# Attention tiles of a two-layer transformer kernel: two tiles of look-ahead, a stacked rope query, joined context tiles, narrower weight splits

## The chip, the cores and the metric

One NeuronCore of a Trainium2 chip runs the whole program. The metric is the device time in microseconds (us) of one execution.

## The reference, cut to what matters

Two layers act on 512 latent tokens (`h`) and 256 context tokens (`g`), model width 1024, in float32. Each layer is: gated feed-forward, a mixer, gated feed-forward, each behind a modulated RMS norm. Layer 0's mixer is the attention in question; layer 1's is a retention, and layer 1 updates only the latents in the end.

```
q = qk_norm(rms_norm(cq) @ w_uq)            # 8 heads, 128 "nope" + 64 "rope" columns
k = qk_norm(rms_norm(ckv) @ w_ukv), k_rope shared by all heads
s = einsum(q, k) * 192 ** -0.5              # nope part + rope part
p = softmax(s); y = (p @ v) @ w_o
# latents: 512 queries over 768 keys (context and latents)
# context: 256 queries over the 256 context keys
```

## The kernel before, in words

Everything is held transposed (features on partitions, tokens along the free dimension). To keep float32 accuracy at the fast matmul format, each operand is split into a high part, rounded by ScalarE (ACT), and a low part, the rest, computed by VectorE (DVE). `three()` (L303) then issues three matmuls: low x high, high x low, high x high. Weights stream in units of 128x2048 through two slots `s0`, `s1`: SyncE loads `raw[s]`, ACT's `split_hi` (L888) writes `wh[s]`, DVE's `split_lo` (L1271) writes `wl[s]` and signals `w_ready[s]`, on which TensorE (PE) waits and after which SyncE loads the next unit.

There is no planner: the order of work is written out by hand in one block for each engine, and semaphores tie the blocks together. The attention stands in `pair()`, once in each block, for four pairs of heads. A pair has three stages.

1. **Items.** PE projects five items (rope queries of both heads, nope queries of each head, nope keys of each head: `project`) and the values. Each item is copied and squared by ACT (`item_square`), summed by PE (`item_sum`, L319), rooted by ACT (`root`), inverted by DVE (`inverse`, L1564), spread over the partitions by PE (`item_spread`, L333), scaled by DVE (`scaled`, L1570), and split (`hi` L1068, `lo` L1576). The rope query of both heads is one tile: head 0 on partitions 0 to 63, head 1 on 64 to 127. It takes one `hi` and one `lo`, into `qrr[:, 0]` and `qrr[:, 1]`. The rope key `krr` holds the same 64 rows twice, and is made once.
2. **Tiles.** Twelve tiles of 128 queries: for each head context queries 4 and 5, then latent queries 0 to 3. Of each tile: `scores` (PE, a `three` of 128 rows and a `three` of the 64 rope rows for each bank of keys); `maximum` (DVE, L1614); `exponent` (ACT, L1113, into one of two rows of `nrm`, with the sum); `diagonal` (DVE, L1621 and L1622, the identity times 1/sum); `turn` (PE, L625, transposes and weights by a matmul with that diagonal); `turned` (ACT L1119 and L1121, then DVE L1627 and L1630, the split of the result into `pt`). `weigh` multiplies by the values, `attended` splits the output. PE issues scores one tile ahead of `turn`; scores of tile n+2 reuse the PSUM banks of tile n and wait for `exp_done` of n; every `turn` waits for `pt_ready` of the tile before it.
3. **Output.** `project_out` for 8 blocks of 512 latents over three PSUM banks, added into `h` by DVE (L1373), then `project_ctx`. `wo_used`, after its first half, lets ACT split the next pair's first unit. PE waits for that unit's `w_ready` at the start of the next pair.

The attention's weight units fill 1152, 1024 or 1024 of the 2048 columns (query, key/value and output weights); some splits are already `1024` wide, others take all 2048.

Of the kernel before, what the change touches and what calls it, by code (L numbers as in the profile page):

```python
# [54 lines left out]
W_BANKS = (0, 3, 2, 5)  # L55
# [48 lines left out]
def build(nc, weights, ada0, ada, c_rows, vecs, consts, x_in, rope_mla, rope_ret, dist_in, out):  # L104
    with ExitStack() as ctx:
# [23 lines left out]
        row = sb("row", [P, 3, 2])  # L129
# [59 lines left out]
        vv = [t[:, 3072:4608].rearrange("p (k e) -> p k e", k=6) for t in xf]  # L189
        oo = [t[:, 4608:6144].rearrange("p (j t) -> p j t", j=2) for t in xf]  # L190
# [108 lines left out]
        def _(pe):  # L299
# [302 lines left out]
            tiles = [(hh, q) for hh in range(2) for q in (4, 5, 0, 1, 2, 3)]  # L602

            def scores(n, hh, q):

                if n >= 2:
                    pe.wait_ge(exp_done, c.next(exp_done))
                b = 2 * (n % 2)
                qs = slice(q * P, q * P + P)
                for t0, n_key in (STREAMS if q < 4 else STREAMS[1:]):  # L610
                    bank = ps[:, b + (t0 > 0), 0:n_key]
                    ks = slice(t0, t0 + n_key)
                    half = slice(ROPE * hh, ROPE * hh + ROPE)
                    three(bank, (qn[:, 0, hh, qs], qn[:, 1, hh, qs]), (kn[:, 0, hh, ks], kn[:, 1, hh, ks]), True, False)
                    ins = three(bank, (qrr[:, 0, qs], qrr[:, 1, qs]), (krr[:, 0, ks], krr[:, 1, ks]), False, True, half)
                ins.then_inc(s_full, 1)

            def turn(n, hh, q):


                pe.wait_ge(p_done, c.next(p_done))
                if n >= 1:
                    pe.wait_ge(pt_ready, c.next(pt_ready))
                for kc in (range(6) if q < 4 else (4, 5)):
                    ins = mm(ps[:, 4 + kc // 4, (kc % 4) * P:(kc % 4) * P + P], nrm[:, n % 2, kc * P:kc * P + P],  # L625
                             nrm[:, 2, (n % 2) * P:(n % 2) * P + P], start=True, stop=True)
                ins.then_inc(pt_full, 1)

            def weigh(hh, part):

                keys = (4, 5) if part == 2 else range(6)
                q0, bank, at = ((0, 6, 0), (L, 6, L), (L, 7, 0))[part]
                for kc in keys:
                    ins = three(ps[:, bank, at:at + L], (vv[0][:, kc, hh * DV:hh * DV + DV], vv[1][:, kc, hh * DV:hh * DV + DV]),
                                (pt[0][:, kc, q0:q0 + L], pt[1][:, kc, q0:q0 + L]), kc == keys[0], kc == keys[-1])
                if part:
                    ins.then_inc(o_full, 1)
# [3 lines left out]
            def pair(first=False, last=False):  # L641
# [52 lines left out]
                scores(0, *tiles[0])  # L694
                for n, (hh, q) in enumerate(tiles):
                    if n == 5:
                        pe.wait_ge(item_ready, c.next(item_ready))
                    if n + 1 < len(tiles):
                        scores(n + 1, *tiles[n + 1])
# [3 lines left out]
                    if q == 1:  # L703
                        weigh(hh, 2)
                    if q == 3:
                        weigh(hh, 0)
                    if q == 4 and hh == 1:
                        pe.wait_ge(pt_ready, c.ahead(pt_ready, 1))
                        weigh(0, 1)
                    turn(n, hh, q)  # L710
                    if q == 0 and hh == 1:
                        pe.wait_ge(o_ready, c.next(o_ready, 2))

                def project_out(m, kk):

                    if kk == 0 and m >= 3:
                        pe.wait_ge(y_added, c.next(y_added))
                    ins = three(ps[:, A_BANKS[m % 3], :], w((s0, s1)[kk], m * P),
# [20 lines left out]
                for m, kk in ((0, 1), (1, 1)) + tuple((m, kk) for m in range(2, KD) for kk in range(2)):  # L739
                    project_out(m, kk)  # L740
                for odd in range(2):
# [8 lines left out]
                c.next(y_added, 3)  # L750
# [5 lines left out]
            with c.loop(pe, PAIRS - 2, {w_ready[0]: 2, w_ready[1]: 2, item_v: 5, item_sq: 5, item_inv: 5,  # L756
                                        item_ready: 5, item_rot: 1, v_ready: 3, exp_done: 12, p_done: 12, pt_ready: 12, o_ready: 4,
# [126 lines left out]
        def _(act):  # L884
# [203 lines left out]
            split_hi(s1)  # L1088
# [10 lines left out]
            split_hi(s0)  # L1099
# [6 lines left out]
            tiles = [(hh, q) for hh in range(2) for q in (4, 5, 0, 1, 2, 3)]  # L1106

            def exponent(n, hh, q):
                act.wait_ge(max_done, c.next(max_done))
                b, e = n % 2, n % 2  # L1110
                cols = (0, T) if q < 4 else (S, T)
                flat = ps[:, 2 * b:2 * b + 2, :].rearrange("p b t -> p (b t)")
                fn(nrm[:, e, cols[0]:cols[1]], flat[:, cols[0]:cols[1]], ACT.Exp, bias=row[:, 0, b:b + 1],  # L1113
                   accum_out=row[:, 1, b:b + 1]).then_inc(exp_done, 1)

            def turned(n, hh, q):
                act.wait_ge(pt_full, c.next(pt_full))
                if q < 4:
                    fn(pt[0][:, 0:4, q * P:q * P + P], ps[:, 4, :].rearrange("p (k q) -> p k q", k=4), ACT.Copy)  # L1119
                q0 = q * P if q < 4 else L + (q - 4) * P  # L1120
                fn(pt[0][:, 4:6, q0:q0 + P], ps[:, 5, 0:256].rearrange("p (k q) -> p k q", k=2), ACT.Copy  # L1121
                   ).then_inc(pt_hi, 1)
# [8 lines left out]
            def pair(first=False, last=False):  # L1131
# [10 lines left out]
                hi(qrr[:, 0, :], nrm[:, 0, :], item_rot)  # L1142
# [15 lines left out]
                exponent(0, *tiles[0])  # L1158
                hi(kn[:, 0, 1, :], nrm[:, 1, :])
                c.next(item_ready, 3)  # L1160
                for n, (hh, q) in enumerate(tiles):
                    if n + 1 < len(tiles):
                        exponent(n + 1, *tiles[n + 1])
                    if q == 1:
                        attended(hh, 1)
                    if q == 4 and hh == 1:
                        attended(0, 0)
                    turned(n, hh, q)
                    if n == 2:
                        split_hi(s1, 1024)  # L1170
# [5 lines left out]
                split_hi(s0)  # L1176
                act.wait_ge(y_full, c.next(y_full, 2 * KD))
                split_hi(s1)

            pair(first=True)  # L1180
            with c.loop(act, PAIRS - 2, {item_full: 5, item_ms: 5, item_v: 5, item_ready: 5, item_rot: 1, v_full: 3, max_done: 12,
                                         pt_full: 12, o_full: 4, wo_used: 1, y_full: 16, raw_full[0]: 32, raw_full[1]: 32}):
                pair()
# [83 lines left out]
        def _(dve):  # L1267
# [117 lines left out]
            def last_y(layer, k, s, parts=STREAMS, early=None):  # L1385

                coefs(layer, k)
                for m in range(KD):
                    add_part(m, parts[0], A_BANKS[m % 3])
# [196 lines left out]
            split_lo(s1)  # L1586
# [9 lines left out]
            for k in range(3):  # L1596
                if k < 2:
                    scaled(k, g[:, k:k + 1], k == 0, pre_kv)
                if k == 1:
                    split_lo(s0)  # L1600
# [6 lines left out]
            tiles = [(hh, q) for hh in range(2) for q in (4, 5, 0, 1, 2, 3)]  # L1607

            def maximum(n, hh, q):
                dve.wait_ge(s_full, c.next(s_full))  # L1610
                b = n % 2
                cols = (0, T) if q < 4 else (S, T)
                flat = ps[:, 2 * b:2 * b + 2, :].rearrange("p b t -> p (b t)")
                nc.vector.tensor_reduce(row[:, 0, b:b + 1], flat[:, cols[0]:cols[1]], AX_X, ALU.max, negate=True  # L1614
                                        ).then_inc(max_done, 1)

            def diagonal(n, hh, q):

                dve.wait_ge(exp_done, c.next(exp_done))
                b = n % 2  # L1620
                step(nc.vector.reciprocal(row[:, 2, b:b + 1], row[:, 1, b:b + 1]))  # L1621
                ts(nrm[:, 2, b * P:b * P + P], ident, row[:, 2, b:b + 1], None, ALU.mult).then_inc(p_done, 1)  # L1622

            def turned(n, hh, q):
                dve.wait_ge(pt_hi, c.next(pt_hi))
                if q < 4:
                    tt(pt[1][:, 0:4, q * P:q * P + P], ps[:, 4, :].rearrange("p (k q) -> p k q", k=4),  # L1627
                       pt[0][:, 0:4, q * P:q * P + P].bitcast(F32), ALU.subtract)
                q0 = q * P if q < 4 else L + (q - 4) * P
                tt(pt[1][:, 4:6, q0:q0 + P], ps[:, 5, 0:256].rearrange("p (k q) -> p k q", k=2),  # L1630
                   pt[0][:, 4:6, q0:q0 + P].bitcast(F32), ALU.subtract).then_inc(pt_ready, 1)
# [9 lines left out]
            def pair(first=False, last=False):  # L1641
# [8 lines left out]
                lo(qrr[:, 1, :], qrr[:, 0, :], nrm[:, 0, :])  # L1650
# [17 lines left out]
                maximum(0, *tiles[0])  # L1668
                value(2)
                for n, (hh, q) in enumerate(tiles):  # L1670
                    diagonal(n, hh, q)
                    if n == 0:
                        lo(kn[:, 1, 1, :], kn[:, 0, 1, :], nrm[:, 1, :])
                    if n + 1 < len(tiles):
                        maximum(n + 1, *tiles[n + 1])
                    if n == 2:
                        split_lo(s0, 1024)
                    if n == 4:
                        split_lo(s1, 1024)
                    if q == 1:  # L1680
                        attended(hh, 1)
                    if q == 4 and hh == 1:
                        attended(0, 0)
                    turned(n, hh, q)
# [4 lines left out]
                for m in range(KD):  # L1689
                    add_part(m, STREAMS[0], A_BANKS[m % 3])  # L1690
                add_pair(0, STREAMS[1], W_BANKS)
                split_lo(s0)
                for m in (2, 4, 6):
                    add_pair(m, STREAMS[1], W_BANKS)
                split_lo(s1)

            pair(first=True)
            with c.loop(dve, PAIRS - 2, {item_std: 5, item_hi: 5, item_swapped: 1, v_hi: 3, s_full: 12, exp_done: 12,
                                         pt_hi: 12, o_hi: 4, y_full: 16, w_hi[0]: 2, w_hi[1]: 2, item_rms: 5,
# [252 lines left out]
```

## Time and profile before

| | before |
|---|---|
| median of 3 runs | 3191.51 us (3191.02 to 3193.46) |
| the profiled execution's own time | 3189.59 us |
| its span, first to last instruction | 3187.9 us |
| PE busy | 3075.0 us, 96% |
| DVE busy | 1820.9 us, 57% |
| ACT busy | 864.7 us, 27% |
| attention, pairs 1 to 4 | about 679 to 1109 us of the span |

Lines of a timeline are: start in us, duration in us, engine, line, operation, operands, count, and in brackets the idle time of the engine before it with what ended it. Durations of pipelined matmuls overlap, so the distance from start to start is the cost in a stream. `wl`, `xnl` and so on name memory, which the attention reuses: `xnh`/`xnl` hold `pt`, the values and the attention output.

### The profile page before, as it was taken

Reading aid. Unit: us, or ns where it says so; the run is one execution under the profiler, and the core shown is the slowest. Engines: PE = TensorE matmul, PEld = TensorE weight load, DVE = VectorE, ACT = ScalarE, POOL = GpSimd, SP = SyncE. Lnnn points to the kernel's source line nnn. Section 1 sums busy time; section 2 is a strip of 40 time slices with the busy share of each in tenths; the row PEclk is TensorE's granted clock in tenths of the full one; section 3 lists DMA queues with packets and bytes.
Section 4 is the critical chain, followed back from the end, with each engine's and each line's share of the span. In section 5 each row is a group of like instructions: output and inputs, shape, how many; then the busy total and the mean of one; then the engine's idle time right before and its main releaser. Section 6 shows DMA issues by size and latency. Waiting matters only on the chain.

```text
span 3187.9 us, 42477 instructions
## 1 busy us (share of the span) xinstructions
PE 3075.0 (96%) x17592; PEld 2638.7 (83%) x17592; DVE 1820.9 (57%) x2652; ACT 864.7 (27%) x1188; POOL 36.7 (1%) x73
## 2 busy tenths in 40 slices
PE   6999999999999899999999999999899999999999
PEld 4888888877777788888888888888788888888887
DVE  4675565864565576655565365656654546454444
ACT  3211121343443431111223111112322223242221
POOL 0000000000000000000000000000000000000000
PEclk8999999999999999999999999999899999999999
DMA  6332322111010043323221132322111212122222
GB/s 241 133 132 99 112 105 92 53 47 53 27 53 27 30 156 119 119 93 118 105 92 54 66 110 97 112 106 87 53 48 59 79 39 79 40 80 94 97 94 84
DMA packets 40984, 277.81 MB, mean 87 GB/s; under 512 B 4352, under 2 KB 5632, under 8 KB 8000
## 3 DMA queue, kind: packets, MB, share of 16 engines
q1 hardware_dynamic: 31024, 205.85, 17.8%
q0 software_dynamic: 9872, 70.72, 6.2%
q8 instruction: 64, 1.05, 0.1%
q14 instruction: 24, 0.20, 0.0%
HBM read 274.45 MB, written 2.10 MB: 87 GB/s over the span
## 4 chain that ended last, share of the span: by engine, by line
PE 90%; DVE 6%; ACT 2%; issue 1%; DMA 0%; SPq 0%; DVEq 0%; ACTq 0%
PE ps L305 29%; PE ps L306 28%; PE ps L307 28%; PE ps L625 2%; PE ps L333 1%; DVE wl L1273 1%; ACT wh L891 1%; DVE act_buf L1357 1%; DVE xnl L1361 1%; PE ps L319 0%; DMA ada_w<-ada 0%; PE ps L351 0%; ACT xnh L922 0%; DVE nrm L1570 0%; PE ps L418 0%
## 5 line engine op out<-in xcount | busy, mean ns | idle before, releaser
L305 PE MATMUL ps<-xnh,wl 128*128 128x512 f32 (+1 forms) x3040 | 1062.5, 350 | 31.4 <-DVE wl L1273 15.6
L306 PE MATMUL ps<-xnl,wh 128*128 128x512 f32 (+1 forms) x3040 | 1052.3, 346 | 0.0
L307 PE MATMUL ps<-xnh,wh 128*128 128x512 f32 (+1 forms) x3040 | 1051.7, 346 | 0.0
L305 PEld LDWEIGHTS ps<-xnh,wl 128*128 128x128 f32 x3040 | 580.7, 191 | 113.7 <-DVE wl L1273 17.5
L307 PEld LDWEIGHTS ps<-xnh,wh 128*128 128x128 f32 x3040 | 580.9, 191 | 70.8
L306 PEld LDWEIGHTS ps<-xnl,wh 128*128 128x128 f32 x3040 | 581.2, 191 | 68.2 <-issue 1.0
L1273 DVE TENSOR_TENSOR wl<-raw,wh 128x2048 fp32r<-128x2048 f32 (+1 forms) x183 | 410.3, 2242 | 145.3 <-ACT wh L891 145.1
L891 ACT ACTIVATE wh<-raw 128x2048 fp32r<-128x2048 f32 (+1 forms) x178 | 332.7, 1871 | 578.8 <-PE ps L307 578.8
L1415 DVE SCALAR_TENSOR_TENSOR h<-ps,coef,h 128x512 f32<-128x512 f32 x624 | 371.7, 642 | 116.1 <-PE ps L307 115.5
L305 PE MATMUL ps<-hidh,wl 128*128 128x512 f32 (+1 forms) x1232 | 425.0, 345 | 3.1 <-DVE h L1373 3.1
L306 PE MATMUL ps<-hidl,wh 128*128 128x512 f32 (+1 forms) x1232 | 426.0, 346 | 0.0
L307 PE MATMUL ps<-hidh,wh 128*128 128x512 f32 (+1 forms) x1232 | 425.2, 345 | 0.0
L1427 DVE TENSOR_TENSOR act_buf<-act_buf,ps 128x512 f32<-128x512 f32 x88 | 60.5, 687 | 542.1 <-ACT act_buf L968 417.0
L966 ACT ACTIVATE act_buf<-ps 128x512 f32<-128x512 f32 x88 | 52.6, 598 | 911.7 <-PE ps L307 911.6
L305 PEld LDWEIGHTS ps<-hidh,wl 128*128 128x128 f32 x1232 | 231.3, 188 | 36.5 <-DVE h L1373 4.4
L306 PEld LDWEIGHTS ps<-hidl,wh 128*128 128x128 f32 x1232 | 231.4, 188 | 31.6
L307 PEld LDWEIGHTS ps<-hidh,wh 128*128 128x128 f32 x1232 | 231.1, 188 | 31.2
L1286 DVE CUSTOM_DVE_ANT_0 ada_prod<-adaw,c_act 128x1024 f32<-128x1024 f32 x120 | 146.5, 1221 | 2.7 <-ACT c_act L895 1.7
L1286 DVE CUSTOM_DVE_ANT_0 adaw<-adaw,c_act 128x1024 f32<-128x1024 f32 x120 | 146.3, 1219 | 0.0
L305 PE MATMUL ps<-wh,xnl 128*128 128x256 f32 x384 | 109.9, 286 | 12.6 <-DVE rv L1754 12.6
L1432 DVE TENSOR_TENSOR hidl<-act_buf,hidh 128x768 fp32r<-128x768 f32 (+1 forms) x88 | 78.5, 892 | 75.6 <-ACT hidh L971 75.6
L306 PE MATMUL ps<-wl,xnh 128*128 128x256 f32 x384 | 109.3, 285 | 0.0
(233 smaller groups left out, 3056.9 us busy)
## 6 DMA issues: line engine op xcount, KB each, us to landing
raw<-weights SPq DMA_DIRECT2D x183, 1024.0 KB, 4.8
adaw<-ada POOLq DMA_DIRECT2D x64, 1024.0 KB, 5.0
ada_w<-ada SPq DMA_DIRECT2D x8, 1024.0 KB, 20.0
h<-x_in SPq DMA_DIRECT2D x1, 2048.0 KB, 8.6
c_act<-c_rows POOLq DMA_DIRECT2D x2, 1024.0 KB, 5.1
out<-h SPq DMA_DIRECT2D x8, 256.0 KB, 2.0
h<-x_in SPq DMA_DIRECT2D x1, 1024.0 KB, 28.9
cs<-rope_mla POOLq DMA_DIRECT2D x1, 512.0 KB, 3.5
```

The costliest lines, as they stand in the source:

```text
L305: mm(dst, lhs[1][rows], rhs[0][rows], start=first, stop=False)
L306: mm(dst, lhs[0][rows], rhs[1][rows], start=False, stop=False)
L307: return mm(dst, lhs[0][rows], rhs[0][rows], start=False, stop=last)
L333: ins = mm(ps[m * i:m * i + m, bank, a - t0:b - t0], quarter[:, col:col + 1].to_broadcast([P, m]), inv[:, a - g * n:b - g * n], start=True ...
L625: ins = mm(ps[:, 4 + kc // 4, (kc % 4) * P:(kc % 4) * P + P], nrm[:, n % 2, kc * P:kc * P + P], nrm[:, 2, (n % 2) * P:(n % 2) * P + P], st ...
L891: fn(wh[:, s, 0:n], raw[:, s, 0:n], ACT.Copy).then_inc(w_hi[s], 1)
L966: ins = fn(act_buf[:, j, 0:S], ps[:, 3 * j, :], ACT.Silu)
L1273: tt(wl[:, s, 0:n], raw[:, s, 0:n], wh[:, s, 0:n].bitcast(F32), ALU.subtract).then_inc(w_ready[s], 1)
L1286: ins = nc.vector.tensor_tensor_reduce(out=prod, in0=w, in1=c_act[:, j, :], scale=1.0, scalar=0.0, op0=ALU.mult, op1=ALU.add, accum_out=ad ...
L1415: ins = stt(out=h[:, m, t0:t0 + n], in0=ps[:, bank, 0:n], scalar=coef[:, 1, m, i:i + 1], in1=h[:, m, t0:t0 + n], op0=ALU.mult, op1=ALU.add)
L1427: ins = tt(act_buf[:, j, 0:S], act_buf[:, j, 0:S], ps[:, 3 * j + 1, :], ALU.mult)
L1432: tt(hidl[:, par, j, 0:n_tok], act_buf[:, j, 0:n_tok], hidh[:, par, j, 0:n_tok].bitcast(F32), ALU.subtract).then_inc(hid_ready, 1)
```

## The change

- `TILES` has ten entries instead of twelve: a head's two context tiles become one, with one set of banks, one `maximum` instruction, two exponentials, two diagonals, four `turn` matmuls and one copy of each half, into its own memory `ptc` (an unused tail of weight slot 0).
- Scores of tiles 0 and 1 are issued before the loop and those of n+2 in it; the exponentials rotate through three rows (`p_row`). ACT and DVE do `exponent(n+2)`, `maximum(n+2)`, `diagonal(n+1)` around `turned(n)`.
- The rope query is stacked: for head hh, `qrr[:, hh]` holds the high part in the head's own 64 partitions and the low part in the other 64. Two matmuls over 128 rows (key low, key high) take the place of three over 64 rows. The split takes two `hi` and two `lo` instructions.
- `weigh` of latent halves is split in two groups of three key blocks, placed behind other turns.
- `project_out` rotates over four banks, and four of its first halves are issued early instead of two.
- Splits of attention units are 3*384 = 1152 or 1024 wide throughout.

```diff
+TILES = [(hh, q) for hh in range(2) for q in (4, 0, 1, 2, 3)]
+        def p_row(n):
+            return (nrm[:, 0, :], sqb[:], nrm[:, 1, :])[n % 3]
...
-                    ins = three(bank, (qrr[:, 0, qs], qrr[:, 1, qs]), (krr[:, 0, ks], krr[:, 1, ks]), False, True, half)
+                    mm(bank, qrr[:, hh, qs], krr[:, 1, ks], start=False, stop=False)
+                    ins = mm(bank, qrr[:, hh, qs], krr[:, 0, ks], start=False, stop=True)
...
-                scores(0, *tiles[0])
-                for n, (hh, q) in enumerate(tiles):
-                    if n == 5:
+                for n in range(2):
+                    scores(n, *TILES[n])
+                for n, (hh, q) in enumerate(TILES):
+                    if n == 3:
                         pe.wait_ge(item_ready, c.next(item_ready))
-                    if n + 1 < len(tiles):
-                        scores(n + 1, *tiles[n + 1])
+                    if n + 2 < len(TILES):
+                        scores(n + 2, *TILES[n + 2])
                     if n == 0:
                         pe.wait_ge(v_ready, c.next(v_ready, 2))
                         pe.wait_ge(item_v, c.next(item_v))
-                    if q == 1:
-                        weigh(hh, 2)
-                    if q == 3:
-                        weigh(hh, 0)
-                    if q == 4 and hh == 1:
-                        pe.wait_ge(pt_ready, c.ahead(pt_ready, 1))
-                        weigh(0, 1)
-                    turn(n, hh, q)
-                    if q == 0 and hh == 1:
-                        pe.wait_ge(o_ready, c.next(o_ready, 2))
+                    turn(n, hh, q)
+                    if n in (6, 8):
+                        pe.wait_ge(o_ready, c.ahead(o_ready, 1))
+                    if n in (3, 8):
+                        weigh(hh, 0, range(0, 3))
+                    if n in (4, 9):
+                        weigh(hh, 0, range(3, 6))
+                    if n == 5:
+                        weigh(0, 1, range(0, 3))
+                    if n == 6:
+                        weigh(0, 1, range(3, 6))
+                    if n in (1, 6):
+                        weigh(hh, 2)
...
                 project_out(0, 0)
+                project_out(2, 0)
                 pe.wait_ge(pt_ready, c.next(pt_ready))
                 weigh(1, 1)
                 project_out(1, 0)
+                project_out(3, 0)
...
-                hi(qrr[:, 0, :], nrm[:, 0, :], item_rot)
+                act.wait_ge(item_rot, c.next(item_rot))
+                for hh in range(2):
+                    own = slice(ROPE * hh, ROPE * hh + ROPE)
+                    ins = fn(qrr[own, hh, :], nrm[own, 0, :], ACT.Copy)
+                ins.then_inc(item_hi, 1)
...
+                exponent(1, *TILES[1])
+                for n, (hh, q) in enumerate(TILES):
+                    turned(n, hh, q)
+                    if n + 2 < len(TILES):
+                        exponent(n + 2, *TILES[n + 2])
+                    if n == 2:
+                        attended(0, 1)
+                        split_hi(s1, 1024)
+                    if n == 7:
+                        attended(0, 0)
+                        attended(1, 1)
...
-                split_hi(s0)
+                split_hi(s0, 3 * 384)
...
+                lo(kn[:, 1, 1, :], kn[:, 0, 1, :], nrm[:, 1, :])
+                maximum(1, *TILES[1])
+                diagonal(0, *TILES[0])
+                for n, (hh, q) in enumerate(TILES):
+                    if n + 2 < len(TILES):
+                        maximum(n + 2, *TILES[n + 2])
+                    if n + 1 < len(TILES):
+                        diagonal(n + 1, *TILES[n + 1])
+                    turned(n, hh, q)
+                    if n in (1, 3):
+                        split_lo((s0, s1)[n // 2], 1024)
```

## Rows read from the trace of the kernel before

**Rows 1.** The page: busy us, share and instructions of each engine.

```profile
PE 3075.0 (96%) x17592; PEld 2638.7 (83%) x17592; DVE 1820.9 (57%) x2652; ACT 864.7 (27%) x1188; POOL 36.7 (1%) x73
```

**Rows 2.** Windows: length; PE, PEld, DVE, ACT, POOL busy; PEclk; DMA share, GB/s.

```profile
780.00:790.00 10.00, 7.11 (x38) 6.25 (x38) 7.72 (x10) 3.71 (x2) 0.00 (x0) 0.83 0.32 105
...
1000.00:1010.00 10.00, 7.03 (x45) 5.71 (x44) 6.84 (x8) 5.38 (x7) 0.00 (x0) 1.00 0.44 133
...
928.00:985.00 57.00, 52.56 (x325) 41.45 (x324) 30.34 (x66) 21.81 (x51) 0.00 (x0) 1.00 0.10 37
```

**Rows 3.** Waits of PE, 676 to 1130 us: total us, times, longest.

```profile
PE ps L305 <- DVE wl L1273: 13.1, 4, 4.3
PE ps L305 <- DVE xnl L1630: 9.8, 8, 1.3
PE ps L625 <- DVE nrm L1622: 5.3, 8, 0.8
...
PE ps L305 <- DVE xnl L1636: 3.0, 4, 0.8
```

**Rows 4.** Timeline of PE: one latent tile's scores, a turn, context scores, weighing.

```profile
943.67 0.48 PE L305 MATMUL ps<-kn,qn 128*128 128x512 f32 x1
...
945.44 0.38 PE L305 MATMUL ps<-kn,qn 128*128 128x256 f32 x1
...
946.53 1.60 PE L625 MATMUL ps<-nrm 128*128 128x128 f32 x12
947.89 0.36 PE L305 MATMUL ps<-kn,qn 128*128 128x256 f32 x1
...
948.97 0.39 PE L305 MATMUL ps<-xnh,xnl 128*128 128x256 f32 x1
```

**Rows 5.** Timeline of PE: first projection after a pair boundary, and the next.

```profile
1003.04 0.51 PE L305 MATMUL ps<-cqn,wl 128*128 128x512 f32 x1 [2.97 <-DVE wl L1273]
...
1006.31 0.39 PE L305 MATMUL ps<-cqn,wl 128*128 128x512 f32 x1
```

**Rows 6.** Timeline of PE: a turn, and the weighing that waits for its split.

```profile
951.23 1.50 PE L625 MATMUL ps<-nrm 128*128 128x128 f32 x12
...
954.74 0.39 PE L305 MATMUL ps<-xnh,xnl 128*128 128x256 f32 x1 [1.12 <-DVE xnl L1630]
```

**Rows 7.** Lines by form, 928 to 985 us: count, busy us, mean ns, idle before.

```profile
L1614 DVE TENSOR_REDUCE row<-ps 128x1 f32<-128x768 f32 x8 | 7.7, 958 | 2.5 <-PE ps L307 2.5
...
L1273 DVE TENSOR_TENSOR wl<-raw,wh 128x1024 fp32r<-128x1024 f32 x2 | 2.4, 1214 | 0.0
...
L1113 ACT ACTIVATE nrm<-ps,row 128x256 f32<-128x256 f32 x4 | 1.9, 475 | 6.0 <-DVE row L1614 6.0
...
L891 ACT ACTIVATE wh<-raw 128x1024 fp32r<-128x1024 f32 x1 | 1.1, 1067 | 0.0
```

**Rows 8.** Timeline of PE and DVE: the first tile's scores, and its maximum.

```profile
927.76 0.42 PE L305 MATMUL ps<-kn,qn 128*128 128x256 f32 x1
...
929.15 0.41 DVE L1614 TENSOR_REDUCE row<-ps 128x1 f32<-128x256 f32 x1
```

**Rows 9.** Timeline of all engines: the rope query's split, and the next spread.

```profile
912.93 0.84 ACT L1068 ACTIVATE qrr<-nrm 128x768 fp32r<-128x768 f32 x1 [1.09 <-DVE nrm L1583]
...
913.80 0.96 DVE L1576 TENSOR_TENSOR qrr<-nrm,qrr 128x768 fp32r<-128x768 f32 x1 [0.91 <-ACT qrr L1068]
...
915.80 1.35 DVE L1564 RECIPROCAL irms<-irms 128x192 f32<-128x192 f32 x1
...
917.31 1.59 PE L333 MATMUL ps<-irms,mats 128*128 128x192 f32 x10
```

**Rows 10.** Timeline of ACT and DVE: splits at the end of pair 3.

```profile
998.75 3.71 ACT L891 ACTIVATE wh<-raw 128x2048 fp32r<-128x2048 f32 x2 [15.02 <-PE ps L307]
...
1000.70 2.29 DVE L1273 TENSOR_TENSOR wl<-raw,wh 128x2048 fp32r<-128x2048 f32 x1 [0.79 <-ACT wh L891]
```

**Rows 11.** Timeline of PE: the spread at the start of pair 1.

```profile
676.40 2.65 PE L333 MATMUL ps<-irms,mats 128*128 128x192 f32 x10 [1.88 <-DVE irms L1564]
```

More of the change, by code:

```diff
@@ L128, in build @@
         lg = sb("lg", [P, 7, 8])
-        row = sb("row", [P, 3, 2])
+        row = sb("row", [P, 3, 2, 2])
         eps = sb("eps", [P, 1])
@@ L600, in _ @@
             slot = s1
-            tiles = [(hh, q) for hh in range(2) for q in (4, 5, 0, 1, 2, 3)]
             def scores(n, hh, q):
@@ L736, in pair @@
                 project_out(1, 0)
+                project_out(3, 0)
                 pe.wait_ge(w_ready[s1], c.next(w_ready[s1]))
                 pe.wait_ge(o_ready, c.next(o_ready, 2))
-                for m, kk in ((0, 1), (1, 1)) + tuple((m, kk) for m in range(2, KD) for kk in range(2)):
+                for m, kk in tuple((m, 1) for m in range(4)) + tuple((m, kk) for m in range(4, KD) for kk in range(2)):
                     project_out(m, kk)
+                pe.wait_ge(y_added, c.next(y_added, 2))
                 for odd in range(2):
@@ L749, in pair @@
                         project_ctx(m, 1)
-                c.next(y_added, 3)
+                c.next(y_added, 2)
                 if not last:
@@ L1104, in _ @@
             slot = s1
-            tiles = [(hh, q) for hh in range(2) for q in (4, 5, 0, 1, 2, 3)]
             def exponent(n, hh, q):
                 act.wait_ge(max_done, c.next(max_done))
[L1110 to L1114, printed above, removed]
+                b = n % 2
+                if q < 4:
+                    flat = ps[:, 2 * b:2 * b + 2, :].rearrange("p b t -> p (b t)")
+                    ins = fn(p_row(n), flat[:, 0:T], ACT.Exp, bias=row[:, 0, b, 0:1], accum_out=row[:, 1, b, 0:1])
+                else:
+                    for i in range(2):
+                        ins = fn(p_row(n)[:, L * i:L * i + L], ps[:, 2 * b + i, 0:L], ACT.Exp, bias=row[:, 0, b, i:i + 1],
+                                 accum_out=row[:, 1, b, i:i + 1])
+                ins.then_inc(exp_done, 1)
             def turned(n, hh, q):
@@ L1157, in pair @@
                 value(2)
-                exponent(0, *tiles[0])
+                exponent(0, *TILES[0])
                 hi(kn[:, 0, 1, :], nrm[:, 1, :])
                 c.next(item_ready, 3)
[L1161 to L1166, printed above, removed]
+                exponent(1, *TILES[1])
[7 more added lines that the diff above has]
+                    if n == 7:
                         attended(0, 0)
-                    turned(n, hh, q)
-                    if n == 2:
-                        split_hi(s1, 1024)
+                        attended(1, 1)
                 attended(1, 0)
@@ L1388, in last_y @@
                 for m in range(KD):
-                    add_part(m, parts[0], A_BANKS[m % 3])
+                    add_part(m, parts[0], A_BANKS[m % 3] if early is None else O_BANKS[m % 4])
                     if m >= 2:
@@ L1605, in _ @@
             slot = s1
-            tiles = [(hh, q) for hh in range(2) for q in (4, 5, 0, 1, 2, 3)]
             def maximum(n, hh, q):
@@ L1611, in maximum @@
                 b = n % 2
[L1612 to L1615, printed above, removed]
+                if q < 4:
+                    out_, in_ = row[:, 0, b, 0:1], ps[:, 2 * b:2 * b + 2, :].rearrange("p b t -> p (b t)")[:, 0:T]
+                else:
+                    out_, in_ = row[:, 0, b, :], ps[:, 2 * b:2 * b + 2, 0:L]
+                nc.vector.tensor_reduce(out_, in_, AX_X, ALU.max, negate=True).then_inc(max_done, 1)
             def diagonal(n, hh, q):
                 dve.wait_ge(exp_done, c.next(exp_done))
-                b = n % 2
-                step(nc.vector.reciprocal(row[:, 2, b:b + 1], row[:, 1, b:b + 1]))
-                ts(nrm[:, 2, b * P:b * P + P], ident, row[:, 2, b:b + 1], None, ALU.mult).then_inc(p_done, 1)
+                b, parts = n % 2, 1 if q < 4 else 2
+                step(nc.vector.reciprocal(row[:, 2, b, 0:parts], row[:, 1, b, 0:parts]))
+                for i in range(parts):
+                    at = (2 * b + i) * P
+                    ins = ts(nrm[:, 2, at:at + P], ident, row[:, 2, b, i:i + 1], None, ALU.mult)
+                ins.then_inc(p_done, 1)
             def turned(n, hh, q):
@@ L1649, in pair @@
                 rotated(0)
-                lo(qrr[:, 1, :], qrr[:, 0, :], nrm[:, 0, :])
+                dve.wait_ge(item_hi, c.next(item_hi))
+                for hh in range(2):
+                    own, other = (slice(ROPE * g, ROPE * g + ROPE) for g in (hh, 1 - hh))
+                    ins = tt(qrr[other, hh, :], nrm[own, 0, :], qrr[own, hh, :].bitcast(F32), ALU.subtract)
+                ins.then_inc(item_ready, 1)
                 scaled(1, gate_cols["qg_nope"])
@@ L1667, in pair @@
                 scaled(1, gate_cols["kg_nope"])
-                maximum(0, *tiles[0])
+                maximum(0, *TILES[0])
                 value(2)
[L1670 to L1675, printed above, removed]
-                    if n == 2:
[L1677 to L1682, printed above, removed]
+                lo(kn[:, 1, 1, :], kn[:, 0, 1, :], nrm[:, 1, :])
[9 more added lines that the diff above has]
+                        split_lo((s0, s1)[n // 2], 1024)
+                    if n == 2:
+                        attended(0, 1)
+                    if n == 7:
                         attended(0, 0)
-                    turned(n, hh, q)
+                        attended(1, 1)
                 attended(1, 0)
```

89 lines of the change are left out of this document (52 added, 37 removed).

## The prediction, made before the changed kernel ran

> **What bounds the kernel now.** I read the page's busy times first: PE is busy 96% of the span and no other engine is near that [rows 1]. So a change pays by PE work that it removes, or by PE waits. The change touches only the four attention pairs, so I then took the windows. A pair's tile stage lasts about 57 us, and in it PE is busy 52.6, DVE 30.3 and ACT 21.8 [rows 2]. The reader should see there that PE is the bound of this stage too, with 4 to 5 us of waiting. The waits of PE name these [rows 3]: over four pairs 9.8 us for a turned tile's split (L1630), 5.3 for a diagonal (L1622), 3.0 for an attention output (L1636) and 13.1 for weights (L1273; three pair boundaries of about 2.9 and one of 4.3 before the next feed-forward). The last view is the timeline of PE, for what one tile costs.
>
> **Scores.** One latent tile runs from 943.67 to 946.53, 2.86 us, and one context tile from 947.89 to 948.97, 1.08 us [rows 4]. A plain stream, without the 64-row form, makes nine matmuls of 512 columns and nine of 256 in 1003.04 to 1006.31, 3.27 us, of which about 0.11 is the first one's start; one of each is (3.27 - 0.11) / 9 = 0.351 us [rows 5]. Twelve matmuls at that rate would be 6 x 0.351 = 2.11, so the tile has a surplus of 0.75: the six matmuls of the first bank alone, 943.67 to 945.44, take 1.77 [rows 4] against 6 x 0.234 = 1.40, and the 64-row form is what sets them apart from a plain stream. After the change a latent tile has five matmuls for each bank, all over 128 rows: 5 x 0.351 + 0.08 for its start = 1.83. I take the surplus as gone, since tensors change elsewhere without it: saved 1.03 a tile, 8.2 for eight. The context tiles go from 4 x 1.08 = 4.3 to two of ten 256-column matmuls at a third of 0.351, 2 x (1.17 + 0.1) = 2.5: saved 1.8. Together 10.0 us a pair. The turns keep their matmuls (a latent turn is 946.53 to 947.89, 1.36 us [rows 4]), and so does the weighing, whose four groups become seven: 3 x 0.1 = 0.3 lost.
>
> **Waits in the tile stage.** Before, a pair waits 9.8/4 + 5.3/4 + 3.0/4 (the last attention output, L1636) = 4.5 us [rows 3]. The new ones follow from one length: a latent turn starts at 951.23, its split is ready at 954.74 [rows 6]. That is 3.5, less the turn's own 1.25 to 1.36, so 2.25 us must be covered by other PE work between two turns. In the new order it is covered by scores (1.83) and half a weighing (9 matmuls of 256 columns, 1.1 to 1.2) for most turns. It is not before turn 3 (context scores alone, 1.27: waits 1.0), before turn 8 (nothing: waits 2.25) and before turn 9 (half a weighing: 1.1). Behind a context turn the split is one ACT and one DVE instruction, about 1.5, and scores cover it. The end, attended output against two early `project_out` halves instead of one, leaves about 0.15 of 0.75.
>
> The start is worse than now. Scores 0 start at 927.76 and DVE's first maximum at 929.15, since the item before it has to be scaled first [rows 8]. From there the new order runs on DVE and ACT: maximum of 512 columns about 0.7 (768 take 0.96 [rows 7]), two exponentials 2 x 0.475 [rows 7], key `hi` 0.83 and `lo` 0.96 (the same forms as the rope query's 0.84 and 0.96 [rows 9]), maximum 1 0.96, reciprocal and two diagonals about 0.8, hand-overs 0.1: 5.3. So turn 0 can start 1.4 + 5.3 = 6.7 us after scores 0. PE has 1.27 + 2 x 1.83 = 4.9 to do: it waits 1.8. The sum of new waits is 1.8 + 1.0 + 2.25 + 1.1 + 0.15 = 6.3, which is 1.8 more than now.
>
> DVE's own load stays below PE's: a latent tile costs it 0.96 + 0.5 + 1.0 = 2.5 against PE's 1.83 + 1.36 + 1.1. The third exponential row lets `exponent(n+2)` be written while `turn(n)` may still read row n; with this order it is a condition, and I cost it at nothing. The splits of the output weights sit on DVE (1.2 each [rows 7]) behind turned 1 and 3, where scores and weighing cover them; without that cover each would cost its 1.2. Four output banks instead of three cost and save nothing, as none of PE's waits here is on an addition [rows 3]. The new wait for two additions ahead of the context projection has two later blocks, 12 x 0.234 = 2.8 us, to hide it; what stands behind it is that projection and the next pair.
>
> **The rope query's split.** Two `hi` instead of one, and two `lo` after both. ACT's takes 0.84 and ends at 913.77, DVE's starts at 913.80 and takes 0.96 [rows 9]; half the partitions do not shorten such an instruction if its time goes by its 768 columns, which no row here shows. That bounds the cost between 0 (time goes by partitions) and 0.84 + 0.96 = 1.8. What is next late is the spread at 917.31 [rows 9]: the inverse that it needs ran from 915.80 to 917.15, ending 0.16 before it [rows 9]. So nearly all arrives at PE, and I take 1.6.
>
> A pair therefore gains 10.0 - 0.3 - 1.8 - 1.6 = 6.3, four pairs 25.2 us.
>
> **Narrower splits.** At the end of a pair ACT splits two full units in 3.71, 1.86 each, and DVE takes 2.29 [rows 10]; at 1024 columns they take 1.07 and 1.21 [rows 7]. At 1152 that makes 1.2 and 1.37: 0.66 + 0.92 = 1.6 a boundary, all of it inside PE's wait of 2.97 [rows 5], which remains with 1.4. Three boundaries: 4.8. Ahead of pair 1 a full split becomes 1024 wide in front of the inverse for which PE waits 1.88 [rows 11]: 0.8 + 1.08, taken as 1.8. The wait of 4.3 before the feed-forward is a full unit's and stays. DMA moves the same units.
>
> **The clock.** Around the first boundary the granted clock averages 0.83 over 10 us [rows 2], that is a third of it at 1.2 GHz and the rest at 2.4, at a price of about 1.7 us; the second boundary shows the same and the third (1.00 [rows 2]) does not, though PE idles equally. Shorter boundary gaps may give back 3; the new waits of 1.8 and 2.25 may cause falls of their own. I take two such falls against two saved: nothing.
>
> **Sum.** 25.2 + 4.8 + 1.8 = 31.8. The profiled execution took 3189.6 and would take 3157.8; the median shown is 1.9 above it, so 3159.5.
>
> **The rivals.**
> 1. *Less waiting than I wrote* (0.17). The split by halves may be half as long, and the first maximum may run early. Without the rope cost (6.4) and the start's wait (7.2) the time is 3146. For: PE's order leaves room in both. Against: the two orders of DVE and ACT are fixed.
> 2. *Turned splits late* (0.15). On DVE `maximum(n+2)` and `diagonal(n+1)` stand in front of `turned(n)`, and on ACT `exponent(n+1)`. If they are not done when a turn ends, 2.25 becomes up to 3.7. That would add 0.7 at five covered turns and 1.45 at three bare ones, 7.9 a pair: 31 in all, no gain left. At half of that the time is 3175. Against: by the rows these instructions have been released when the turn starts.
> 3. *The surplus of the scores stays* (0.06). If 0.75 a tile belongs to something else than the 64-row form, scores save only a matmul a bank: 8 x 0.351 + 4 x 0.117 = 3.3 a pair. Then pairs lose 0.4 each and 3186.5 remains, within what can be told from no change. The Trainium skill (TensorEngine Tiling (Array Packing), Key Properties) says that changing the tiling mode drains TensorE, which speaks against this rival. The same page (Theoretical Speedup) says that a contraction of up to 64 rows can run up to twice as fast. By that, three 64-row matmuls would cost 1.5 full ones, fewer than the two that replace them, and scores would lose 0.18 a tile. The trace disagrees: the 64-row threes are longer, not shorter.
> 4. *The clock falls* (0.04), and the result is slower. Place: the tail of each pair, where waits of 2.25, 1.1 and 1.4 now follow each other. Each us of work at 1.2 GHz loses half a us. The point of decision is 2 x (31.8 + 6.4) / 4 = 19 us a pair at the lower level. With all of the 36 us from turn 8 to the next pair's first projections at 1.2 GHz, 18 x 4 = 72 is lost and the time is 3231. Against: in the tile stage the clock stays at 1.00 through waits of up to 1.3 [rows 2, 3]. The Trainium skill (TensorE: Matmul & The Clock Gate, A second HAM failure mode) describes this, frequent short idles between groups of matmuls that make the clock oscillate; here only falls beside the longer waits are seen.
>
> **The numbers.** The forecast has 0.58, its own range 3152 to 3167 (rope split 0 to 1.8, some falls more or fewer). The whole range, 3146 to 3176, takes in rivals 1 and the half of 2. About 0.2%, 6.4 us, is what a measurement of this kernel tells from no change. Faster by more: forecast, 1 and 2, 0.90; within: rival 3, 0.06; slower: rival 4, 0.04.
>
> **What would show it.** Right: a latent tile's scores in 1.8 us with even steps of 0.234 and 0.117; PE waits of about 1.8 on L1622's successor once a pair, about 2.25 once; boundary waits near 1.4; a new wait of about 1.5 ahead of a spread in the item stage. Wrong: more than 8 us of waits in a tile stage (rival 2), scores still above 2.3 (rival 3), PEclk below 0.9 in tile windows (rival 4), or rope copies of 0.5 us (rival 1).

## The result, and the profile after

The changed kernel takes 3135.35 us (median of 4 runs, 3134.22 to 3136.25); the kernel before, measured beside it, 3191.9. The ratio is 0.9823, 95% interval 0.9807 to 0.9838. Forecast were 3159.5 and 3146 to 3176: the direction is right, the gain of 56 us is far more than the 32 forecast. The span of the profiled execution fell from 3187.9 to 3134.2, by 53.7 us.

The page answers to [rows 1] with:

```profile
PE 3019.6 (96%) x17512; PEld 2624.0 (84%) x17512; DVE 1811.6 (58%) x2632; ACT 859.2 (27%) x1184; POOL 36.7 (1%) x73
```

Where the time went is best read by cutting both traces at the same matmuls. The attention stretch runs from the last matmul of the first feed-forward on its hidden activations (`hidh`) to the first such one of the next feed-forward:

| stretch, in us | before | after | less | forecast |
|---|---|---|---|---|
| first matmuls to 606.86 / 605.12 | 606.9 | 605.1 | 1.7 | 0 |
| the attention stretch, to 1186.93 / 1144.69 | 580.1 | 539.6 | 40.5 | 31.8 |
| the three feed-forwards and the retention behind it, to the start of the last matmul | 1997.4 | 1985.9 | 11.5 | 0 |

So 13 us are saved in code that the diff does not touch, and 9 more than forecast in the attention. The windows of the attention stretch, with columns as in [rows 2], divide its part. First the kernel before, then the changed one:

```profile
606.86:1186.93 580.07, 535.64 (x3339) 439.73 (x3338) 352.31 (x588) 240.02 (x462) 4.20 (x8) 0.98 0.15 54
605.12:1144.69 539.57, 494.03 (x3259) 430.22 (x3258) 343.22 (x568) 234.44 (x458) 4.21 (x8) 0.98 0.16 58
```

PE is busy 41.6 us less, where the forecast's terms make 38.8, and idle 1.1 us more, where they make 7.0. So of the 9 us about 6 are waits that did not come, and 3 are PE work.

The timeline of PE in the third pair shows that the tiles themselves came out as worked out:

```profile
900.90 0.41 PE L311 MATMUL ps<-kn,qn 128*128 128x256 f32 x1
...
907.50 0.68 PE L635 MATMUL ps<-nrm 128*128 128x128 f32 x4 [1.26 <-DVE nrm L1653]
...
908.39 0.48 PE L311 MATMUL ps<-kn,qn 128*128 128x512 f32 x1
...
910.23 1.50 PE L630 MATMUL ps<-nrm,sqb 128*128 128x128 f32 x12
...
917.64 1.58 PE L630 MATMUL ps<-nrm 128*128 128x128 f32 x12 [0.92 <-DVE xnl L1660]
...
938.25 2.13 PE L630 MATMUL ps<-nrm 128*128 128x128 f32 x12 [2.11 <-DVE xnl L1660]
...
965.59 0.51 PE L311 MATMUL ps<-cqn,wl 128*128 128x512 f32 x1 [1.29 <-DVE wl L1303]
```

A latent tile's scores take 910.23 - 908.39 = 1.84 us (forecast 1.83, before 2.86). Turn 0 starts 6.6 after scores 0 (forecast 6.7). Turns 3 and 8 wait 0.92 and 2.11 (1.0 and 2.25), the boundary 1.29 (1.4). The waits of PE, 600 to 1110 us, answer to [rows 3]; columns are us in total, times, longest. The five waits for `wl` take in one of 0.9 us ahead of pair 1, which the window of [rows 3] leaves out:

```profile
PE ps L630 <- DVE xnl L1660: 13.9, 12, 2.1
PE ps L311 <- DVE wl L1303: 8.9, 5, 4.3
PE ps L339 <- DVE irms L1594: 8.6, 8, 1.8
PE ps L635 <- DVE nrm L1653: 5.0, 4, 1.3
```

### The profile page after: what moved, and what is told of

Same layout as the page of the kernel before. It is cut to its first block, busy times and chain, and to the rows that moved or that the text cites. A ratio compares the mean times of both kernels' runs of the same rounds, so it can differ in the third digit from the quotient of the medians.

```text
span 3134.2 us, 42265 instructions
## 1 busy us (share of the span) xinstructions
PE 3019.6 (96%) x17512; PEld 2624.0 (84%) x17512; DVE 1811.6 (58%) x2632; ACT 859.2 (27%) x1184; POOL 36.7 (1%) x73
## 4 chain that ended last, share of the span: by engine, by line
PE 88%; DVE 7%; ACT 2%; issue 2%; DMA 0%; SPq 0%; DVEq 0%; ACTq 0%
PE ps L311 28%; PE ps L313 28%; PE ps L312 28%; PE ps L630 2%; PE ps L339 1%; DVE wl L1303 1%; DVE act_buf L1387 1%; ACT wh L913 1%; DVE xnl L1391 1%; DVE irms L1594 0%; PE ps L325 0%; DVE ssum L1366 0%; DMA ada_w<-ada 0%; PE ps L357 0%; ACT xnh L944 0%
## 5 line engine op out<-in xcount | busy, mean ns | idle before, releaser
L1303 DVE TENSOR_TENSOR wl<-raw,wh 128x2048 fp32r<-128x2048 f32 (+2 forms) x183 | 402.3, 2199 | 142.0 <-ACT wh L913 141.7
L913 ACT ACTIVATE wh<-raw 128x2048 fp32r<-128x2048 f32 (+2 forms) x178 | 326.7, 1835 | 564.8 <-PE ps L313 564.8
```

The costliest lines, as they stand in the source:

```text
L913: fn(wh[:, s, 0:n], raw[:, s, 0:n], ACT.Copy).then_inc(w_hi[s], 1)
L1303: tt(wl[:, s, 0:n], raw[:, s, 0:n], wh[:, s, 0:n].bitcast(F32), ALU.subtract).then_inc(w_ready[s], 1)
```

## The experiments

Labels e1 to e12 are runs of their own; times are medians of 4 to 7 runs, each beside 9 to 11 runs of the kernel before on the same chip (3189.8 beside e1 to e4, 3191.4 beside e5 to e8, 3191.5 beside e9 to e12).

**The 13 us outside.** In feed-forward code both programs issue the same matmuls. The timeline of PE in the second feed-forward, before:

```profile
1599.95 0.28 PE L305 MATMUL ps<-hidh,wl 128*128 128x256 f32 x1
...
1600.30 0.39 PE L305 MATMUL ps<-hidh,wl 128*128 128x512 f32 x1
...
1600.99 0.39 PE L305 MATMUL ps<-hidh,wl 128*128 128x512 f32 x1
```

and after:

```profile
1599.93 0.39 PE L311 MATMUL ps<-hidh,wl 128*128 128x512 f32 x1
...
1600.62 0.28 PE L311 MATMUL ps<-hidh,wl 128*128 128x256 f32 x1
...
1600.96 0.28 PE L311 MATMUL ps<-hidh,wl 128*128 128x256 f32 x1
...
1601.30 0.39 PE L311 MATMUL ps<-hidh,wl 128*128 128x512 f32 x1
```

Three 256-column matmuls take 0.35 us before and 0.34 after, three of 512 columns 0.69 each time here. Over all of them the median distance falls from 117 to 113 ns (256 columns) and from 233 to 229 (512), while the same matmuls on the normalised activations (`xnh`, `xnl`; xn below) stay at 120 and 227. One thing differs: `row` grew from 24 to 48 bytes a partition, and every tensor allocated after it starts 32 bytes further in memory (adding up the allocations, `hidh` starts 64 bytes past a multiple of 128 instead of 32); `xnh` and the weights stand before it.

```diff
         row = sb("row", [P, 3, 2])
+        pad = sb("pad", [P, 8])
```

> The kernel before with one unused tensor of 32 bytes a partition behind `row`, so that every tensor allocated after `row` starts 32 bytes further, as in the changed kernel; nothing else. Theory A (placement): the part of the gain that shows outside the attention, about 12 us, comes from the new shape of `row`, which moves the hidden activations, the retention's scores and the attention's queries and keys from starts that are 32 bytes past a multiple of 64 to multiples of 64; matmuls that stream them then run about 2% closer together. It expects 12 to 20 us less than before, 3172 to 3180, with the distance between hidden-activation matmuls falling from about 187 to 184 ns. Rival B (the two programs differ by where their code lies, or by the executions compared): within 3 us of before.

Measured: 3177.6, ratio 0.996 (0.9947 to 0.9974), 12.2 us less. The attention stretch stays (580.5 against 580.1), what is behind it falls from 1997.4 to 1986.0, as in the changed kernel, and the distances are its 113 and 229. Theory A holds at its lower end.

> The changed kernel with the same unused 32 bytes behind `row`, which puts the later tensors back to starts 32 bytes past a multiple of 64. Theory A expects it 12 to 20 us slower than the changed kernel, 3147 to 3155. Rival B expects 3135.

Measured: 3154.0 (the same `pad` in the changed kernel), 18.7 us more than the changed kernel; 119 and 232 ns. So 32 bytes of placement alone are worth 12 us in one program and 19 in the other. The two steps are not the same one: e1 goes from 32 to 64 bytes past a multiple of 128, e2 from 64 to 96, and not back to 32.

**The rope query.** e3 is the changed kernel with the old rope lines of the diff on PE, ACT and DVE; e4 the kernel before with the new ones.

```diff
-                    mm(bank, qrr[:, hh, qs], krr[:, 1, ks], start=False, stop=False)
-                    ins = mm(bank, qrr[:, hh, qs], krr[:, 0, ks], start=False, stop=True)
+                    half = slice(ROPE * hh, ROPE * hh + ROPE)
+                    ins = three(bank, (qrr[:, 0, qs], qrr[:, 1, qs]), (krr[:, 0, ks], krr[:, 1, ks]), False, True, half)
```

> The changed kernel with the rope query as before: one high and one low copy, three matmuls over 64 rows for each bank. By the prediction's sum the stack saves 8 x 1.03 + 1.8 = 10.0 us less 1.6 a pair of matmul time and copies, so that without it the time is up to 34 us longer, 3169; since longer scores also cover waits of 0.9 and 1.3 us a pair that exist only because scores are short, 25 to 30 us is expected, 3160 to 3165. Rival (the look-ahead and the order carry the gain): less than 12 us.

Measured: 3160.7, 25.4 more than the changed kernel; the attention stretch is 563.5 instead of 539.6. A latent tile's scores are back at 2.88 us:

```profile
912.47 0.50 PE L311 MATMUL ps<-kn,qn 128*128 128x512 f32 x1
...
913.03 0.40 PE L313 MATMUL ps<-kn,qn 128*128 128x512 f32 x1
913.36 0.50 PE L311 MATMUL ps<-krr,qrr 64*128 64x512 f32 x1
913.70 0.39 PE L312 MATMUL ps<-krr,qrr 64*128 64x512 f32 x1
913.93 0.39 PE L313 MATMUL ps<-krr,qrr 64*128 64x512 f32 x1
914.25 0.39 PE L311 MATMUL ps<-kn,qn 128*128 128x256 f32 x1
...
915.35 0.50 PE L311 MATMUL ps<-kn,qn 128*128 128x512 f32 x1
```

The distances in the middle are 0.33, 0.34, 0.23 and 0.32 us. The surplus is thus about 0.1 us at each of the steps into, behind and out of the 64-row group; between two 64-row matmuls behind that, the distance is the 0.23 of full rows.

> The kernel before with the stacked rope query alone (two high and two low copies, two matmuls over 128 rows), the rest of its tile order kept: one tile ahead, twelve tiles, two exponential rows. If the stack carries the gain whatever the order, 25 us less than before, 3167. If the old order needs the longer scores as a cover, every latent turn waits about 2.26 - 1.83 = 0.4 us more and every context tile about 1 us, and 5 to 15 us are left, 3177 to 3187; I expect the latter.

Measured: 3179.5, ratio 0.9971 (0.996 to 0.9982), 10.3 less than before. The seven runs fall into two groups, 3178.0 to 3179.5 (four, mean granted clock 0.992 to 0.994) and 3183.6 to 3187.2 (three, 0.988 to 0.989), so the gain is 3 to 12 us. The stack is worth 25 us in the new order and about 10 in the old one, where longer scores were the cover of the turns' chain: in e4's profiled execution (one of the longer group) PE's waits for a diagonal are 24.3 us in 28 times, against 5.3 in 8 before. The two values also stand at different placements (e3 has the changed kernel's, e4 that of before).

**The narrower splits.**

```diff
-                split_hi(s0, 3 * 384)
+                split_hi(s0)
```

and so on for the other seven of the diff's narrowed splits (four on ACT and four on DVE in all).

> The changed kernel with the attention units' splits that were full before taking all 2048 columns again. By the prediction's sum 1.6 us for each of three pair boundaries and 1.8 ahead of pair 1 are lost again, 6.6: 3142. Rival (the narrower splits also let other waits go, or save falls of the clock at the boundaries, 1.5 us each): 10 us or more, 3145 and above.

Measured: 3149.0, 13.7 more, and on the rival's side. The waits on the weights' low part are 14.0 instead of 8.9 and those on L1594 11.4 instead of 8.6, 7.9 together, near the sum. In the attention stretch (13.6 more) the rest is 1.7 us of waits on L1660 and 4 us of PE's own time, and both fit the clock. The windows of 10 us behind the first two boundaries are these, columns as in [rows 2]:

```profile
773.83:783.83 10.00, 10.00 (x51) 8.27 (x52) 5.41 (x8) 4.29 (x9) 0.00 (x0) 0.83 0.60 211
876.20:886.20 10.00, 9.98 (x51) 8.23 (x52) 5.42 (x8) 4.28 (x9) 0.00 (x0) 0.83 0.57 210
```

and of the changed kernel, behind its first boundary, then around two of its bare turns:

```profile
768.33:778.33 10.00, 10.00 (x61) 8.42 (x62) 4.78 (x8) 4.87 (x10) 0.00 (x0) 1.00 0.59 211
836.00:846.00 10.00, 7.67 (x52) 7.28 (x51) 4.74 (x11) 3.87 (x9) 0.00 (x0) 0.83 0.00 0
935.00:945.00 10.00, 7.70 (x54) 7.28 (x53) 4.58 (x11) 4.25 (x10) 0.00 (x0) 0.83 0.00 0
```

With full splits a third of the window is at 1.2 GHz behind boundaries, where PE has dense projections: 51 matmuls in 10 us against 61. All matmuls on `cqn` together keep PE busy for 44.6 us there and 39.8 in the changed kernel (43.5 before). The falls of 3.4 us that the trace of e5 shows before the end of pair 4 are six: one ahead of pair 1, one behind each of the three boundaries, and one at turn 8 of pairs 2 and 3. The changed kernel has four: at turn 8 of pairs 2, 3 and 4, and one at a spread in pair 4's items. At turn 8 half is absorbed: the turn grows from 1.58 to 2.13 or more, and the wait before turn 9 shrinks from 1.04 (pair 1, no fall) to 0.2 to 0.4.

```profile
745.23 1.58 PE L630 MATMUL ps<-nrm 128*128 128x128 f32 x12 [1.04 <-DVE xnl L1660]
...
942.48 1.59 PE L630 MATMUL ps<-nrm 128*128 128x128 f32 x12 [0.19 <-DVE xnl L1660]
```

**Everything but the tiles.** e6 is e4 with the `pad` of e1 and the narrow splits.

> The kernel before with the 32-byte shift, the stacked rope query and the narrower splits, but its own twelve tiles, one tile ahead, and its own output banks. If the parts add up, it takes before - 12 (shift) - 10 (stack in the old order) - 7 (splits) = 3161 to 3163, and the new tile order with its joined context tiles is worth the remaining 26 us to the changed kernel. Rival (the tile order as such brings little, as its new waits eat what the look-ahead saves): below 3145.

Measured: 3156.1, ratio 0.9891 (0.9876 to 0.9906), 5 to 7 less than the parts' sum; its trace has no fall of the clock between the first feed-forward and pair 4's end, where the kernel before has four. What e6 lacks, the order of tiles and weighings with the joined context tiles and the four output banks, is worth the other 21 us. Its turns wait often, as e4's expectation said:

```profile
PE ps L626 <- DVE nrm L1627: 24.1, 28, 1.6
PE ps L306 <- DVE xnl L1635: 11.0, 8, 1.4
```

**Filling the waits.** Three edits on the changed kernel: DVE's start, the place of two weighings (with their waits for `o_ready`), and a signal for each half of the rope query.

```diff
-                lo(kn[:, 1, 1, :], kn[:, 0, 1, :], nrm[:, 1, :])
-                maximum(1, *TILES[1])
                 diagonal(0, *TILES[0])
+                maximum(1, *TILES[1])
+                lo(kn[:, 1, 1, :], kn[:, 0, 1, :], nrm[:, 1, :])
...
-                    if n == 6:
+                    if n == 7:
                         weigh(0, 1, range(3, 6))
-                    if n in (1, 6):
+                    if n in (1, 7):
                         weigh(hh, 2)
...
-                    ins = fn(qrr[own, hh, :], nrm[own, 0, :], ACT.Copy)
-                ins.then_inc(item_hi, 1)
+                    fn(qrr[own, hh, :], nrm[own, 0, :], ACT.Copy).then_inc(item_hi, 1)
```

> The changed kernel with three waits attacked: the first diagonal ahead of the second maximum and the key's low part on DVE (turn 0 waits 1.26 in each pair); the second half of the weighing of head 0 and head 1's context weighing behind turn 7 instead of 6 (turn 8 waits 2.1, which should fall to 0.4, with 0.4 new before turn 7); the two halves of the rope query's split signalled one by one, so that DVE starts on the first while ACT does the second (0.75). By rows that is about 1.2 + 1.3 + 0.75 = 3.2 us a pair, 13 in all: 3122. Rival (the gaps only move, or the chain of item norms sets the item stage): less than 6 us.

Measured: 3118.9, ratio 0.9774 (0.976 to 0.9787): 16 us less than the changed kernel, the best version of the study. Its waits:

```profile
PE ps L630 <- DVE xnl L1659: 10.6, 16, 1.0
PE ps L311 <- DVE wl L1302: 9.0, 5, 4.3
PE ps L339 <- DVE irms L1593: 5.8, 9, 0.9
```

The wait for the first diagonal is gone, and that on the splits of turned tiles is never over 1.0. The attention stretch is 17.1 us shorter; PE's idle time in it falls by 11, not by the 13 worked out, and its busy time by 6. No fall of the clock is left between the first feed-forward and pair 4's end. Four falls of 3.4 us at half the clock are up to 7 us, which fits those 6; that they are the cause is not shown by a run of its own.

**What of the placement decides.** Five more layouts, each by unused tensors alone; e10 to e12 are based on e8.

> The changed kernel with 64 unused bytes behind `row`: tensors allocated after it start at multiples of 128 bytes instead of 64 past one. So far starts at 64 past a multiple of 128 gave 113 ns between 256-column hidden-activation matmuls, 32 past gave 117 and 96 past gave 119. If only the multiple of 64 matters, the time is within 2 us of the changed kernel. If each step counts, it differs by 3 us or more; which way is open.

> The changed kernel with 128 unused bytes behind `row`, so that the later tensors again start 64 past a multiple of 128, but 128 bytes further. So far: 32 past gives 117 ns between 256-column hidden-activation matmuls, 64 past 113, 96 past 119 to 120, a multiple of 128 gives 117 to 118. If the place within 128 bytes decides, the time is the changed kernel's within 2 us (3135) and the distance 113. If the absolute place or the distance to the weights decides, it differs by 4 us or more.

> e8 with the normalised activations moved too: 64 unused bytes ahead of `h` and 64 ahead of `raw`, so that `xnh`/`xnl` start 64 past a multiple of 128 (they were at a multiple), weights and all later tensors stay at their place within 128 bytes. If the rule holds for them, 256-column matmuls on xn go from 120 to about 114 ns; there are about 3900 in a stream, so up to 23 us less than e8, 3096 to 3110. If the 512-column ones (227 ns now, against 229 of the hidden activations) go to 229, 10 us of it are lost again. Rival (hidden activations are a case of their own): 3119 within 2.

> e8 with `raw`, `wh`, `wl` moved 64 bytes (64 past a multiple of 128), activations all where e8 has them. If the relation between the streamed operand and the loaded weights decides, hidden-activation matmuls fall back to 117 ns and xn matmuls gain, and both distances change; if the streamed operand's own place decides, both stay (113 and 120) and the time is 3119 within 2 us.

> e8 with everything at 64 past a multiple of 128: 64 unused bytes ahead of `h`, 64 behind `row`. If only the streamed operand's place decides, it equals e10. If the relation to the weights decides, it equals e8 with hidden-activation matmuls at 117.

Starts are bytes past a multiple of 128; distances are medians in ns for 256 and 512 columns:

| kernel | `xnh` | weights | `hidh` | xn | hidden | time |
|---|---|---|---|---|---|---|
| before | 0 | 0 | 32 | 120, 227 | 117, 233 | 3191.9 |
| changed, e1, e8 | 0 | 0 | 64 | 120, 227 | 113 to 114, 229 to 230 | 3135.4, 3177.6, 3118.9 |
| e2 | 0 | 0 | 96 | 120, 227 | 119, 232 | 3154.0 |
| e7 | 0 | 0 | 0 | 120, 227 | 117, 232 | 3146.8 |
| e9 | 0 | 0 | 64, 128 further | 120, 227 | 114, 233 | 3142.8 |
| e10 | 64 | 0 | 64, 128 further | 113, 233 | 118, 230 | 3134.9 |
| e11 | 0 | 64 | 64, 128 further | 113, 234 | 117, 232 | 3139.4 |
| e12 | 64 | 64 | 64, 128 further | 120, 227 | 117, 232 | 3133.2 |

For the xn matmuls the relation decides, not the place: 64 bytes apart from the weights (e10, e11) gives 113 and 233, none apart gives 120 and 227 wherever both stand (e8, e12). That is a loss here, as the kernel has 5232 of 512 columns and 3888 of 256. For the hidden activations neither the relation within 128 bytes nor the absolute place explains all rows: e9 has that of the changed kernel within 128 and is 7 us slower, and e10 has its exact distance to the weights and still 118. So e11 and e12 come out as the branch of their expectations that goes by the relation to the weights (e12 is e8 with the hidden activations back at 117), and e7, with the same relation as these two, has their 117 and 232 (its expectation named no such branch; it is 11.5 us off the changed kernel, so the multiple of 64 is not all). e9 and e10 contradict a relation within 128 bytes. e10 missed every branch of its expectation: 3134.9, where 3096 to 3110 or 3119 was expected, since the 512-column matmuls on xn lost more than the others gained, and the hidden activations lost too. No single rule of those stated covers all rows; what mechanism stands behind them stays open, and nothing further was tried.

## Why the prediction was wrong

- **Scores.** Right: 1.84 us a tile. The surplus went with the 64-row form, and rival 3 is out: without the stack 25 us are lost (e3). The Trainium skill's rule of up to twice the speed (TensorEngine Tiling (Array Packing), Theoretical Speedup) finds no support in e3, where the shortest distance of 64-row matmuls, 0.23 us, is that of full ones.
- **Waits of the tile stage.** Right in place: 1.26, 0.92, 2.11, 1.04 in pair 1 against 1.8, 1.0, 2.25, 1.1. Too high in sum: 25.2 us were forecast for four pairs, and 13.9 + 5.0 = 18.9 came. The first wait is 0.5 shorter in each pair, and the one before turn 9 nearly vanishes where the clock falls at turn 8. These 6 us are most of the 9 by which the attention gained more. Rival 2 is out, and so is rival 1 in its first half, the cheap rope split; its second half, an early start, came true for a third of its 7.2 us.
- **The rope query's split.** Right: both halves of the partitions take the full time, here two copies in 1.69 and two differences in 1.92, and the next spread waits 1.59 (forecast 1.6).

```profile
884.23 1.69 ACT L1170 ACTIVATE qrr<-nrm 64x768 fp32r<-64x768 f32 x2 [1.10 <-DVE nrm L1613]
...
885.95 1.92 DVE L1686 TENSOR_TENSOR qrr<-nrm,qrr 64x768 fp32r<-64x768 f32 x2 [1.76 <-ACT qrr L1170]
...
890.36 1.69 PE L339 MATMUL ps<-irms,mats 128*128 128x192 f32 x10 [1.59 <-DVE irms L1594]
```

- **Narrower splits and the clock.** The waits were 7.9 against 6.6. "Two such falls against two saved: nothing" came out in count, four falls before pair 4's end in either kernel, but the place counts: undoing the splits costs 13.7. By `cqn`'s 4.7 us for three falls, one in dense projections costs about 1.5 us; one among waits costs a part of that. Cut the other way, by taking the splits out first, stack and tiles gained 40.5 - 13.6 = 26.9 (e5's stretch is 553.2) instead of 25.2, and the splits with the clock 7 more than forecast.
- **The sum itself.** The step that failed is the silent one: that code which the diff does not touch keeps its time. I read `row`'s new shape as bookkeeping. It moved every later tensor by 32 bytes, worth 12.2 us alone (e1). With it the forecast would have been 3147, and with the measured splits 3140; of the 5 us then left, nearly 3 are that the medians differ by 56.5 and the profiled executions by 53.7. (The sum as written also slips by 0.2: 3157.8 and 1.9 make 3159.7.) The sum has a second fault, that its attention terms are 9 us short, as said above; by itself either would have left the time inside the range. Why 32 bytes matter stays open.
- **Rival 4.** The clock did fall at turn 8 in three of the four pairs, and once at a spread, but returned after 3.4 us each time; its mean is 0.99 in both kernels. The Trainium skill (TensorE: Matmul & The Clock Gate, A second HAM failure mode) describes frequent short idles between groups of matmuls that make the clock oscillate. That is not what these traces show: each fall before pair 4's end in the changed kernel stands beside a wait of 1.79 or 2.11 us, and e6, with 28 waits of up to 1.6 us for diagonals, has none.

## What to carry to other kernels

Before a sum is trusted, list what a diff does to memory: a small tensor that grows moves all that are allocated after it, and the first thing to look at in a result is the time of code that was not touched. Price a wait by what follows it: work that removes PE time also removes the cover of the next chain, so look for turns with nothing between them and move independent matmuls there. A saving and the order that lets it count belong together; here the same edit was worth about 10 us in one order and 25 in the other. And split a stage's gain into busy and idle time before you explain it: the terms of a sum can be off against each other.

## What was not expected of the hardware

The distance between two matmuls of the same form depends on where the operands start in memory: 113 to 120 ns for 256 columns, 227 to 234 for 512, and the two do not move together (64 bytes between `xnh` and the weights: 113 and 233; none: 120 and 227). Over this kernel that is up to 20 us, 0.6% (e11 against e8). The second is that a fall of the granted clock follows waits of 1.8 to 3 us of PE in some pairs and not in others (the 2.11 before turn 8 in pair 1 of the changed kernel has none), and costs least where PE would have waited anyway.
